# Gate and up products with high and low token halves side by side, and the halves added on VectorE

## What is computed

```python
def swiglu(x, w_gate, w_up, w_down):
    return (jax.nn.silu(x @ w_gate) * (x @ w_up)) @ w_down

def macaron_ffn(xs, g, shift, scale, gate, w_gate, w_up, w_down):
    return xs + 0.5 * gate * swiglu(modulate_2(xs, g, shift, scale), w_gate, w_up, w_down)
```

## Time and profile before

| | |
|---|---|
| median of 3 runs | 2091.01 us |
| the profiled execution's own time | 2083.61 us |
| span of that execution | 2081.8 us |
| granted TensorE clock, mean | 0.976 |
| busy: TensorE, weight loads, GpSimd, VectorE, ScalarE | 1976.3, 1777.9, 1397.8, 974.1, 829.1 us |
| share of the chain that ended last on TensorE | 78% |
| from HBM | 471.18 MB |

### The profile page before, as it was taken

One profiled execution on the slowest core, in us unless ns is written; L12 is line 12 of the kernel. 1 busy time (PEld: TensorE's weight loads), 2 busy tenths in 40 slices (PEclk: granted clock), 3 DMA queues, 4 the chain that ended last, 5 costly groups with the idle time before them and its releaser, 6 DMA issues.

```text
span 2081.8 us, 34613 instructions
## 1 busy us (share of the span) xinstructions
PE 1976.3 (95%) x13814; PEld 1777.9 (85%) x13814; DVE 974.1 (47%) x2137; ACT 829.1 (40%) x873; POOL 1397.8 (67%) x325
## 2 busy tenths in 40 slices
PE   6999689999999999999999898899999999999998
PEld 4879666677676799999999768689999999999998
DVE  6676434568575354345335232653335333642112
ACT  4343344344444454344434332443334333424332
POOL 5727188887878667777775313077776777766884
PEclk9999789999999999999999899899999999999999
DMA  8536199999998656665664202066664666554452
GB/s 353 224 122 263 61 357 365 381 362 381 360 388 335 242 214 232 241 239 227 243 238 162 104 21 102 21 225 241 242 242 183 243 241 242 221 184 157 185 183 81
DMA packets 67406, 473.79 MB, mean 228 GB/s; under 512 B 8064, under 2 KB 9184, under 8 KB 10208
## 3 DMA queue, kind: packets, MB, share of 16 engines
q1 hardware_dynamic: 65344, 466.82, 58.8%
q10 hardware_dynamic: 1952, 5.44, 0.7%
HBM read 471.18 MB, written 1.05 MB: 227 GB/s over the span
## 4 chain that ended last, share of the span: by engine, by line
PE 78%; POOL 6%; DVE 5%; issue 5%; DMA 4%; ACT 2%; SPq 0%; ACTq 0%; POOLq 0%; DVEq 0%
PE bank L645 18%; PE bank L647 17%; PE bank L646 17%; PE bank L1115 5%; PE bank L651 3%; PE bank L653 3%; PE bank L652 3%; DMA raw<-in_pages 3%; POOL W L575 3%; POOL YC L627 2%; PE bank L679 2%; PE bank L670 1%; PE bank L700 1%; PE bank L1213 1%; PE bank L701 1%
## 5 line engine op out<-in xcount | busy, mean ns | idle before, releaser
L575 POOL TENSOR_TENSOR W<-raw,W 128x2048 fp32r<-128x2048 f32 x220 | 1014.3, 4615 | 536.0 <-ACT W L1382 536.0
L645 PE MATMUL bank<-YH,W 128*128 128x256 f32 x1936 | 553.7, 286 | 3.9 <-DVE YL L1762 3.6
L646 PE MATMUL bank<-YL,W 128*128 128x256 f32 x1936 | 549.5, 284 | 0.0
L647 PE MATMUL bank<-YH,W 128*128 128x256 f32 x1936 | 549.5, 284 | 0.0
L1382 ACT ACTIVATE W<-raw 128x2048 fp32r<-128x2048 f32 x220 | 420.1, 1910 | 321.6 <-PE bank L647 276.1
L645 PEld LDWEIGHTS bank<-YH,W 128*128 128x128 f32 x1936 | 373.1, 193 | 7.1 <-DVE YL L1762 3.8
L646 PEld LDWEIGHTS bank<-YL,W 128*128 128x128 f32 x1936 | 373.4, 193 | 0.6 <-issue 0.5
L647 PEld LDWEIGHTS bank<-YH,W 128*128 128x128 f32 x1936 | 373.1, 193 | 0.0
L1703 DVE SCALAR_TENSOR_TENSOR bank<-mraw,CA,bank 128x256 f32<-128x256 f32 x702 | 331.4, 489 | 20.3
L1800 DVE TENSOR_TENSOR bank<-bank,SIL 128x256 f32<-128x256 f32 x110 | 47.5, 432 | 573.7 <-ACT SIL L1401 573.7
L645 PE MATMUL bank<-HH,W 128*128 128x256 f32 x880 | 249.4, 283 | 0.4 <-DVE HL L1802 0.4
(11 more groups left out here) (342 smaller groups left out, 3102.2 us busy)
## 6 DMA issues: line engine op xcount, KB each, us to landing
raw<-in_pages SPq DMA_DIRECT2D x300, 1024.0 KB, 4.9
mraw<-in_mpages SPq DMA_DIRECT2D x98, 1024.0 KB, 6.9
R<-in_pages SPq DMA_DIRECT2D x24, 1024.0 KB, 5.1
XR<-in_pages SPq DMA_DIRECT2D x16, 1024.0 KB, 6.2
R<-in_mpages SPq DMA_DIRECT2D x4, 1024.0 KB, 16.5
HT<-in_acts ACTq DMA_DIRECT2D x1, 1024.0 KB, 14.3
CT<-in_mpages SPq DMA_DIRECT2D x1, 1024.0 KB, 19.4
raw<-in_mpages SPq DMA_DIRECT2D x1, 1024.0 KB, 25.2
```

Source lines behind the costliest of these rows:

```text
L575: nc.gpsimd.tensor_tensor(WL[:, p % SLOTS, :], raw[:, p % SLOTS, :], WH[:, p % SLOTS, :].bitcast(f32), ALU.subtract).then_inc(s_lo, 1)
L645: mm(out, w[0], x[0], start=start, stop=False, skip_group_check=True)
L646: mm(out, w[0], x[1], start=False, stop=False, skip_group_check=True)
L647: return mm(out, w[1], x[0], start=False, stop=stop, skip_group_check=True)
```

## The change

For every gate and up page but the first of a pass, the high and low tokens (now two halves of one tensor Y2, or of YC2) are one moving operand of 512 columns for `wh`, into the two halves of a bank; `wl*xh` is added to the second half. Gate has bank 4 and up bank 5, for both pages. VectorE adds the halves with a TENSOR_REDUCE: gate into SIL, on which ScalarE then does the silu in place, and up into the right half of bank 7. Two semaphores (gate_summed, up_summed) let TensorE overwrite the banks, a third (gate_done) tells VectorE that the gate half of a page is there. The first page of a pass keeps matmuls of 256 columns, in the same layout.

```diff
--- before.py
+++ after.py
@@ -114,8 +114,8 @@
         MACC = sb("MACC", [P, 2, 2, FU])
         HT = sb("HT", [P, KD, S])
         CT = sb("CT", [P, KD, S])
-        YH = sb("YH", [P, KD, S], f32r)
-        YL = sb("YL", [P, KD, S], f32r)
+        Y2 = sb("Y2", [P, 2, KD, S], f32r)
+        YH, YL = Y2[:, 0], Y2[:, 1]
         YC2 = sb("YC2", [P, 2, KD, S], f32r)
         YCH, YCL = YC2[:, 0], YC2[:, 1]
         XR = sb("XR", [P, KD, S])
@@ -257,7 +257,7 @@
         s_os, s_sct, s_scd = sem("group_out_copied"), sem("group_scattered"), sem("group_added")
-        s_silu = sem("silu_done")
+        s_gate, s_gsum, s_usum, s_silu = sem("gate_done"), sem("gate_summed"), sem("up_summed"), sem("silu_done")
         s_sq = sem("norm_squares")
         s_rt, s_ri, s_xr, s_yf, s_y = (sem("norm_root"), sem("norm_coef"), sem("norm_scaled"), sem("norm_result"),
                                          sem("norm_split"))
@@ -646,6 +646,11 @@
                 mm(out, w[0], x[1], start=False, stop=False, skip_group_check=True)
                 return mm(out, w[1], x[0], start=False, stop=stop, skip_group_check=True)
 
+            def mm_halves(ps, w, x, start, stop):
+
+                mm(ps[:, :].rearrange("p (a t) -> p a t", a=2), w[0], x, start=start, stop=False, skip_group_check=True)
+                return mm(ps[:, S:2 * S], w[1], x[:, 0, :], start=False, stop=stop, skip_group_check=True)
+
             def mm3x(out, x, w, start, stop):
 
                 mm(out, x[0], w[0], start=start, stop=False, skip_group_check=True)
@@ -723,7 +728,7 @@
 
             def ff_pass(name, norm_of, between=()):
                 p0, u0, n, src, acc, parts = PASSES[name]
-                x = OPERANDS[src]
+                x, wide = OPERANDS[src], {"y": Y2, "yc": YC2}[src]
                 tail = TAIL[name] if name in TAIL else None
                 before(acc)
                 for b in GU:
@@ -736,16 +741,32 @@
                     for j in range(2):
                         w = shaped(arrived(p + j, i), "p (k g n) -> p k g n", k=KD, g=2)
 
-                        pe.wait_ge(s_hid, i * 4 + (2 * U + j + 1))
                         if u == 0 and j == 0:
-                            first_page(norm_of, PS[GU[j]], x, lambda a, k, g: w[a][:, k, g, :]).then_inc(s_page, 1)
+                            for k in range(KD):
+                                pe.wait_ge(s_yf, KD * norm_of + k + 1)
+                                for g in range(2):
+                                    for half in range(2):
+                                        mm(PS[GU[g]][:, half * S:(half + 1) * S], w[half][:, k, g, :], x[0][:, k, :],
+                                           start=(k == 0 and half == 0), stop=False, skip_group_check=True)
+                                y_ready(norm_of, k)
+                                for g in range(2):
+                                    last = mm(PS[GU[g]][:, S:2 * S], w[0][:, k, g, :], x[1][:, k, :], start=False,
+                                              stop=(k == KD - 1), skip_group_check=True)
+                                    if g == 0 and k == KD - 1:
+                                        last.then_inc(s_gate, 1)
+                            last.then_inc(s_page, 1)
                             if name == "ctx_ff":
                                 last_scatter()
                             continue
                         for g in range(2):
+                            if g == 0:
+                                pe.wait_ge(s_gsum, i * 4 + (2 * U + j + 1))
+                            else:
+                                pe.wait_ge(s_usum, i * 4 + (2 * U + j + 1))
                             for k in range(KD):
-                                last = mm3(PS[GU[j]][:, g * S:(g + 1) * S], [a[:, k, g, :] for a in w],
-                                           [a[:, k, :] for a in x], k == 0, k == KD - 1)
+                                last = mm_halves(PS[GU[g]], [a[:, k, g, :] for a in w], wide[:, :, k, :], k == 0, k == KD - 1)
+                            if g == 0:
+                                last.then_inc(s_gate, 1)
                         last.then_inc(s_page, 1)
                     if vectors:
                         for at_unit, ss in MID_NORM[name]:
@@ -1397,8 +1418,8 @@
                     p = p0 + UNIT_PAGES * u
                     for j in range(2):
 
-                        act.wait_ge(s_page, i * 2 * UNIT_PAGES + (p + j + 1))
-                        f(SIL[:, j, :], PS[GU[j]][:, 0:S], ACT.Silu).then_inc(s_silu, 1)
+                        act.wait_ge(s_gsum, i * 4 + (2 * (u0 + u) + j + 2))
+                        f(SIL[:, j, :], SIL[:, j, :], ACT.Silu).then_inc(s_silu, 1)
                         if p + j + SLOTS < RPAGES:
                             split(p + j + SLOTS, i)
                     if p + 2 + SLOTS < RPAGES and not (u == n - 1 and name in TAIL):
@@ -1795,8 +1816,15 @@
                             ins.then_inc(s_hx, 1)
                             dve.wait_ge(s_hx, i * 4 * steps + done[0])
 
+                        gate, up = (PS[b][:, :].rearrange("p (a t) -> p t a", a=2) for b in GU)
+                        sil, hid = SIL[:, j, :], PS[MISC][:, S:2 * S]
+                        dve.wait_ge(s_gate, i * 4 + (2 * U + j + 1))
+                        v.tensor_reduce(sil, gate, AX.X, ALU.add).then_inc(s_gsum, 1)
+                        dve.wait_ge(s_page, i * 2 * UNIT_PAGES + (p0 + UNIT_PAGES * u + j + 1))
+                        dve.wait_ge(s_hid, i * 4 + (2 * U + j + 2))
+                        v.tensor_reduce(hid, up, AX.X, ALU.add).then_inc(s_usum, 1)
+                        dve.wait_ge(s_usum, i * 4 + (2 * U + j + 2))
                         dve.wait_ge(s_silu, i * 4 + (2 * U + j + 1))
-                        sil, hid = SIL[:, j, :], PS[GU[j]][:, S:2 * S]
                         step(v.tensor_tensor(hid, hid, sil, ALU.mult))
                         step(v.tensor_copy(HH[:, j, :], hid))
                         v.tensor_tensor(HL[:, j, :], hid, HH[:, j, :].bitcast(f32), ALU.subtract).then_inc(s_hid, 1)
@@ -1814,6 +1842,8 @@
             v.memset(EPSC[:], EPS).then_inc(sem("eps"), 1)
             v.memset(SIL[:, 0, :], 0.0).then_inc(s_hid, 1)
             v.memset(SIL[:, 1, :], 0.0).then_inc(s_hid, 1)
+            v.memset(ST[:, 0:1], 0.0).then_inc(s_gsum, 1)
+            v.memset(ST[:, 1:2], 0.0).then_inc(s_usum, 1)
             v.memset(MACC[:], 0.0)
             v.memset(ONES[:], 1.0).then_inc(sem("ones"), 1)
             dve.wait_ge(sem("ones"), 1)
```

## The result

The changed kernel takes 2104.26 us (median of 4 runs, 2100.84 to 2105.39) beside 2090.57 us for the kernel before (4 runs): 13.7 us more, a ratio of 1.0062 with a 95% interval of 1.0044 to 1.0079. That is slower, as forecast, but the forecast's step was 6.0 us. The profiled execution took 2103.97 us with a span of 2102.2 us and a mean granted clock of 0.968 (before: 0.976).

What follows compares the result with a forecast made beforehand. TensorE, busy 95% of the span, was taken to bound the kernel. Terms -19.3 + 20.3 + 5.0 = +6.0 us, carried onto the 2091.0 us median, gave 2097.0 us, range 2088.5 to 2112.

Steps and rivals of the forecast that it cites:

- Part 1, the wide matmul: Gate and up pages after each pass's first: 1680 pairs of 512 plus 256 columns save 0.0115 us each, -19.3 us.
- Part 2, hid: End of each unit's page: the added reductions make hid 0.38 us later, still covered before down's second half; 0 us.
- Part 2, the eight waits: Second pages at pass starts and beside norms 3, 4, 5: TensorE waits for the gate's reduction, +20.3 us.
- Part 3, the clock: Behind the longer of these waits TensorE drops to its 1.2 GHz level; +5.0 us, ends 0 and 10.
- What moves and costs nothing: ScalarE's earlier silu starts its page split up to 0.38 us sooner; nothing waits for it, so no cost.
- A: Second pages of ctx_ff unit 3 and ff00 unit 2: clock not lowered after 4.9 us waits; 2092.0 us, chance 0.22.
- B: Gate and up pairs: the 256 behind a 512 runs at bare column rate, saving 0.04 us; 2049.1 us, chance 0.05.
- C: VectorE's reductions: the strided read costs a full second cycle, 1.2 us each; 2100.9 us, chance 0.15.
- D: Gate and up pages: a wide matmul is no cheaper than two narrow ones, no gain; 2116.3 us, chance 0.08.

Runs made afterwards that it cites:

- e7: The changed kernel with each wide matmul split into two of 256 columns again, banks, waits and reductions kept; 2123.21 us, ratio 1.0145 to the kernel before.
- e9: The changed kernel with one more VectorE reduction of 0.70 us per page, result unused, ahead of up's; 2104.39 us, ratio 1.0084 to the kernel before.
- e1: The changed kernel with the halved gate column HG going through PSUM in two small operations; 2094.24 us, ratio 1.0020 to the kernel before.
- e10: The kernel before the change, with HG going through PSUM as a control; 2091.52 us, ratio 1.0008 to the unedited kernel before.

## Why the prediction was right, and where it was not

**Part 1, the wide matmul: -19.3 us, measured -21.3.** Right in mechanism and a little small: 0.0127 us a pair instead of 0.0115, inside its ends. e7 shows it by itself. The 21.3 us are the rate of six units of ctx_ff times 1680, an upper value: unit 4 of ff00 and units 1 and 2 of ff01 gained 0.22 us instead of 0.405.

**Part 2, hid: 0, measured 0.** TensorE has no wait for HL in the changed kernel's list. The reduction takes 0.69 to 0.70 us (forecast 0.8), and e9 shows the cover's edge.

**Part 2, the eight waits: +20.3 us, measured 16.5.** All eight are where the prediction put them, in its order of size (forecast 2.2, 1.2, 4.9, 1.0, 4.9, 2.2, 2.9, 1.0; measured 1.66, 1.31, 4.48, 0.76, 4.38, 1.48, 1.71, 0.76). The forecast's 1.2 us for unit 1 is net of an old wait of 0.36 us that the new one replaces; measured in that way it is 0.95, and the sum 16.1. 0.9 us is the faster reduction. At ff10 the first page ran slower (8.35 us instead of 7.34, clock), so the modulation sum ahead of the reduction was further on when TensorE stopped: in e1, where the page took 7.34 us, the wait was 2.72 us, near the forecast's 2.9.

**Part 3, the clock: +5.0 us (0 to 10), measured about 9.** Behind the two long waits the forecast of 2.0 us each was close. Windows of 4 us behind them:

```profile
795.00:799.00 4.00, 4.00 (x15) 3.45 (x16) 1.74 (x4) 2.14 (x2) 1.79 (x1) 0.63 0.00 0
977.50:981.50 4.00, 4.00 (x13) 3.42 (x14) 1.63 (x4) 2.03 (x2) 1.90 (x1) 0.50 0.00 0
```

By the modulation products of these units (the unit with norm 4: +10.61 to +16.36, with norm 5: +13.69 to +20.35) less the wait and plus the gain of 0.405 us, the clock cost 1.7 and 2.7 us. Another 3.5 us lie behind the two waits for HG, in the squares of norms 8 and 9. The forecast had no price for them, as it did not have the waits; by the earlier trace rows, where 2.15 us of idling left the clock at 1.00, it would hardly have given one. 1.0 us is ff10's first page, and 0.6 us is the balance of two more places between norms 9 and 10 (a first page 0.9 us shorter, and 1.5 us more behind a wait of 2.06 us); all three stand behind waits that the kernel before has too, and the runs cannot say whether they are the change's doing.

**"What moves and costs nothing": this step failed.** It said that the page split starts up to 0.38 us sooner and that nothing waits for it. The split did start 0.28 us sooner. But HG stood 0.51 us ahead of it on another engine, itself became 0.31 us later, and fell behind it. The two waits are 4.8 us and the clock behind them 3.5: 8.3 us at a place that the prediction put at nothing, and 8.8 by the ratio of e1. The prediction looked for those who wait for the moved instruction by a semaphore, and HG waits for it without one. HG's 0.16 us and its distance to the split could be read in the trace of before; that they mattered could be seen there as well. At the end of ctx_ff HG began at 914.80 us in a split of 911.26 to 915.88 us and took 1.10 us, and at the end of ff00 it took 1.09 us in the same way: two times in five, and not once, as e10's expectation has it.

**The rivals.** A (clock not lowered) is out by the two windows. B (narrow matmuls at their column rate) is out: 0.348 us a pair. C (the stride costs) is out: 691 to 698 ns. The Trainium skill's advice on contiguous PSUM pairs ("Advanced Engine Details and Errata", section "PSUM Cachelines") does not show in a reduction that alternates over 1 KB; the measurement decides. D is out by e7.

**The sum:** -21.3 + 16.5 + 4.8 for HG's waits and -0.4 for the old wait at unit 1 make -0.4; the stretch of the passes says +12.1. The difference of 12.5 us is the clock (9.4 us, as above); the other 3 us lie in small steps of the table, such as the units that gained less than 0.405 us, and were not followed up. The time of 2104.3 lay in the range, but it got there by luck: the room above 2097.0 us was meant for a dearer reduction and a lower clock behind the norms, and HG's 8.3 us filled it. The call "slower" owes as much to HG. Without it (e1) the kernel is 4.2 us slower than the one before by the ratio, near the forecast's 6.0 and at the edge of what the prediction called no change.
